# Block compression with stationary blocks over four column strips, and the by-token projection's first unit ahead of the compression's units

## The reference: what is computed

```python
def compress_blocks(k, pe, w1, b1, w2):          # k: (1, 512, 2, 64)
    n_cmp = (T - 32) // 16 + 1                    # 31
    idx = np.arange(n_cmp)[:, None] * 16 + np.arange(32)[None, :]
    blocks = k[:, idx] + pe[None, None, :, None, :]
    flat = transpose(blocks).reshape(B, n_cmp, Hkv, 32 * 64)
    return gelu(flat @ w1 + b1) @ w2              # w1: (2048, 64), w2: (64, 64)

h = rms_norm_2(x, g_pre_mix[l])
q_nsa, kv_nsa, g_nsa, qkv_sb, g_merge = split(h @ w_in)
k_cmp, k_slc, k_win = (rope(kv[:, :, n]) for n in (0, 2, 4))
v_cmp, v_slc, v_win = kv[:, :, 1], kv[:, :, 3], kv[:, :, 5]
o_nsa = gated sum of attention over compressed, selected and window keys
```

## Time and profile before

| | us |
|---|---|
| time, median of 3 runs (2902.05 to 2902.65) | 2902.12 |
| profiled execution | 2901.89 |
| its span, first to last instruction | 2900.1 |
| TensorE busy | 2883.0 (99%) |
| VectorE, ScalarE, GpSimd busy | 1833.0, 1275.3, 182.0 |
| compression on TensorE, first layer | 1384.13 to 1391.72 |
| compression on TensorE, second layer | 2159.77 to 2167.36 |

### The profile page before, as it was taken

One profiled execution on the slowest core, in us unless ns is written; L12 is line 12 of the kernel. 1 busy time (PEld: TensorE's weight loads), 2 busy tenths in 40 slices (PEclk: granted clock), 3 DMA queues, 4 the chain that ended last, 5 costly groups with the idle time before them and its releaser, 6 DMA issues.

```text
span 2900.1 us, 38167 instructions
## 1 busy us (share of the span) xinstructions
PE 2883.0 (99%) x14822; PEld 2384.1 (82%) x14822; DVE 1833.0 (63%) x3171; ACT 1275.3 (44%) x2352; POOL 182.0 (6%) x124
## 2 busy tenths in 40 slices
PE   9999999999999999999999999999999999999998
PEld 7888888888888888888888788888888888888886
DVE  6766775356565487734666768775365777677743
ACT  4544443233333344432366644543333765444431
POOL 1000000010000000000101301000030021100000
PEclk9999999999999999999999999999999999999999
DMA  4233323322222223232411132322333112323222
GB/s 168 74 102 95 102 95 97 99 87 80 80 80 87 95 98 99 95 97 93 136 59 45 59 109 79 103 95 95 101 106 112 43 45 73 109 80 102 95 95 73
DMA packets 74725, 263.88 MB, mean 91 GB/s; under 512 B 9008, under 2 KB 9008, under 8 KB 74416
## 3 DMA queue, kind: packets, MB, share of 16 engines
q1 hardware_dynamic: 73680, 258.03, 27.6%
q10 hardware_dynamic: 864, 3.41, 0.3%
HBM read 255.64 MB, written 2.10 MB: 89 GB/s over the span
## 4 chain that ended last, share of the span: by engine, by line
PE 94%; ACT 2%; DVE 2%; issue 1%; POOL 0%; DVEq 0%
PE bank L552 26%; PE bank L559 26%; PE bank L555 26%; PE bank L765 2%; PE bank L629 2%; PE bank L633 2%; PE bank L630 2%; PE bank L744 2%; PE bank L729 1%; PE bank L935 1%; DVE big L2207 1%; PE bank L720 1%; ACT pp L1162 1%; ACT big L1486 1%; PE bank L988 1%
## 5 line engine op out<-in xcount | busy, mean ns | idle before, releaser
L1507 DVE TENSOR_TENSOR wl<-ring,wh 128x512 fp32r<-128x512 f32 (+1 forms) x928 | 637.3, 693 | 782.4 <-ACT wh L1071 777.0
L552 PE MATMUL bank<-xh,wh 128*128 128x512 f32 x2392 | 942.7, 394 | 0.1
L555 PE MATMUL bank<-xh,wl 128*128 128x512 f32 x2392 | 931.7, 390 | 0.0
L559 PE MATMUL bank<-xl,wh 128*128 128x512 f32 x2392 | 903.8, 390 | 0.0
L1071 ACT ACTIVATE wh<-ring 128x512 fp32r<-128x512 f32 (+1 forms) x928 | 569.0, 622 | 683.3 <-PE bank L559 612.6
L552 PEld LDWEIGHTS bank<-xh,wh 128*128 128x128 f32 x2392 | 449.2, 188 | 101.9 <-issue 10.4
L559 PEld LDWEIGHTS bank<-xl,wh 128*128 128x128 f32 x2392 | 449.0, 188 | 94.5
L555 PEld LDWEIGHTS bank<-xh,wl 128*128 128x128 f32 x2392 | 449.4, 188 | 90.9 <-DVE wl L1507 1.1
L552 PE MATMUL bank<-bigr,wh 128*128 128x512 f32 x1024 | 398.8, 389 | 0.1
L555 PE MATMUL bank<-bigr,wl 128*128 128x512 f32 x1024 | 398.4, 389 | 0.0
L559 PE MATMUL bank<-bigr,wh 128*128 128x512 f32 x1024 | 393.4, 389 | 0.0
(11 more groups left out here) (240 smaller groups left out, 2890.0 us busy)
## 6 DMA issues: line engine op xcount, KB each, us to landing
ring<-in_w_up SPq DMA_DIRECT2D x176, 512.0 KB, 3.5
ring<-in_w_down SPq DMA_DIRECT2D x88, 512.0 KB, 3.4
ring<-in_w_in SPq DMA_DIRECT2D x64, 512.0 KB, 3.5
ring<-in_w_ret SPq DMA_DIRECT2D x32, 512.0 KB, 3.4
ring<-in_w_even SPq DMA_DIRECT2D x19, 512.0 KB, 3.5
ring<-in_w_ret_v SPq DMA_DIRECT2D x16, 512.0 KB, 3.4
ring<-in_w_ret_out SPq DMA_DIRECT2D x16, 512.0 KB, 3.5
ring<-in_w_proj SPq DMA_DIRECT2D x16, 512.0 KB, 3.5
```

What stands on the lines that cost most here:

```text
L552: e.matmul(o, K.wh(p, c * 128, 128), oh, start=start, stop=False, skip_group_check=True)
L555: e.matmul(o, K.wl(p, c * 128, 128), oh, start=False, stop=False, skip_group_check=True)
L559: m = e.matmul(o, K.wh(p, c * 128, 128), ol, start=False, stop=stop, skip_group_check=True)
L1507: e.tensor_tensor(K.wl(i, 0, w), K.raw(i), K.wh(i, 0, w).bitcast(F32), ALU.subtract).then_inc(F.lo.tell(("piece", i)), 1)
```

## The change

The roles in the compression are exchanged. The stationary block is now 64x32: one token offset of the 32 blocks, from a block input `cin(i, part)` that VectorE makes beforehand (tokens plus position table, 32 blocks, the last one zero for part 1). The moving operand is 64 columns of `w1`. The four combinations of keys/values and head write four strips of 32 partitions of one PSUM bank, and the parts are summed there. So `w1` is laid out with the units in the order (keys part 0, values part 0, keys part 1, values part 1), and the compression runs in two halves of 64 instructions, by part. The result has the blocks on the partitions; ScalarE copies it (`hb`), TensorE transposes it behind step 1 of the by-token projection (`hidden_turn`), and ScalarE applies gelu with the bias `b1` straight from PSUM (`hidden_act`). The second layer reads rows 0 to 63 and moves from behind step 3 to behind step 4. VectorE's additions on the small sums go.

In the ring the projection's first unit (pieces 0 to 2) now stands ahead of the four `w1` units; its splits stand in ScalarE's list ahead of the copy, and in VectorE's list behind rope 3 (two) and behind the next scaling (one). The half turns keep their places between the `w1` units.

```diff
@@ weights
-    def moving(self, src, u, key, n, per):
+    def moving(self, src, u, key, n, per, second=None):
         self.first[key] = len(self.pieces)
         for k in range(0, DT, per):
+            if k == per and second is not None:
+                second()
             self.unit(...)
-        for i in range(4):
-            W.raw(D[f"w1_{l}"][i], ("w1", l, i))
-        W.moving(D[f"w_tm{l}"], 0, ("tm", l), 280, 3)
+        W.moving(D[f"w_tm{l}"], 0, ("tm", l), 280, 3, lambda: [W.raw(D[f"w1_{l}"][i], ("w1", l, i)) for i in range(4)])
@@ class Kit
+    def cin(self, i, part):
+        return self.big(11424 + (2 * i + part) * S).rearrange("p (n r) -> p n r", r=16)
@@ sync_program
-        turns.update({u + 1: (l, (0, 1)), u + 2: (l, (2,)), u + 3: (l, (3,)), u + 4: (l, (4,)), u + 7: (l, (5, 6))})
+        turns.update({u + 1: (l, (0, 1)), u + 2: (l, (2,)), u + 3: (l, (3,)), u + 4: (l, (4,)), u + 6: (l, (5, 6))})
@@ tensor_program
-        for i in range(2):
-            c = (K.kcr, K.vcr)[i]
...
-            for part in range(2):
-                u = W.raws["w1", l, 2 * i + part]
-                q.wait_ge(K.landed(u), ("unit", u))
-                for n in range(16):
-                    for kv in range(2):
-                        r = slice(64 * kv, 64 * kv + 64)
-                        m = e.matmul(BK[b][r, 32 * part:32 * part + 32], K.slot(u)[r, n * 64:(n + 1) * 64],
-                                     c[r, 2 * part:2 * part + 32, n], start=part == 0 and n == 0, stop=n == 15,
-                                     skip_group_check=True)
-                m.then_inc(F.attn.tell(("cmp", l, i, part), ("unit", u)), 1)
+        for part in range(2):
+            units = [W.raws["w1", l, 2 * part + i] for i in range(2)]
+            for i in range(2):
+                q.wait_ge(F.dve, ("cin", l, i, part))
+                q.wait_ge(K.landed(units[i]), ("unit", units[i]))
+            for n in range(16):
+                for i in range(2):
+                    for kv in range(2):
+                        r, c = slice(64 * kv, 64 * kv + 64), 64 * i + 32 * kv
+                        m = e.matmul(BK[spare[0]][c:c + 32, 0:64], K.cin(i, part)[r, :, n], K.slot(units[i])[r, n * 64:(n + 1) * 64],
+                                     start=part == 0 and n == 0, stop=part == 1 and n == 15, skip_group_check=True)
+            m.then_inc(F.attn.tell(("cmp", l, part), *[("unit", u) for u in units]), 1)
+        def hidden_turn():
...
+            e.transpose(BK[b][0:64, 0:128], K.hb, K.cs("ident")).then_inc(F.attn.tell(("ch", l)), 1)
-        by_token(("tm", l), 280, s, F.act, {3: compressed})
+        by_token(("tm", l), 280, s, F.act, {1: hidden_turn, 4: compressed})
@@ vector_program
+        def block_input(i):
+            src = (K.KC, K.VCB)[i].rearrange("p (n r) -> p n r", r=16)
+            for part in range(2):
+                a = VEC["pe"] + 64 * l + 32 * i + 16 * part
+                pe = bc(K.VC[:, a:a + 16], [[0, 32 - part], [1, 16]])
+                if part:
+                    e.memset(K.cin(i, part)[:, 31, :], 0.0)
+                e.tensor_tensor(K.cin(i, part)[:, 0:32 - part, :], src[:, part:32, :], pe, ALU.add).then_inc(
+                    F.dve.tell(("cin", l, i, part)), 1)
...
+        block_input(1)
         rope(1)
+        block_input(0)
         rope(2)
         times_rs(K.tmp(0), ("n", l, 6), s, ("ra", l, 5))
         rope(3)
+        lo_to(W.first["tm", l] + 1)
         times_rs(K.tmp(1), ("n", l, 7), s, ("ra", l, 6))
+        lo_to(W.first["tm", l] + 2)
         rope(4)
```

More of the change, by code:

```diff
@@ L336, in memory @@
     K.NQT = [K.big(j * S) for j in range(4)]
-    K.KSL, K.KWN, K.KC, K.VCB = K.big(2048), K.big(2560), K.big(3072, 544), K.big(3616, 544)
-    K.kcr, K.vcr = (t.rearrange("p (n r) -> p n r", r=16) for t in (K.KC, K.VCB))
+    K.KSL, K.KWN, K.KC, K.VCB = K.big(2048), K.big(2560), K.big(3072), K.big(3616)
     K.TM = K.big(4160, 1120)
@@ L344, in memory @@
     K.GM = [K.big(11424 + j * S) for j in range(16)]
-    K.ropes = [K.KC[:, 16:528], *K.NQT, K.KSL, K.KWN]
+    K.ropes = [K.KC, *K.NQT, K.KSL, K.KWN]
     K.at_ropes = [0, S, 2 * S, 3 * S, 2048, 2560]
+    K.hb = K.big(20768, 64)
     K.hid, K.gates = K.big(20640, 128), K.big(20896, 96)
@@ L972, in tensor_program @@
         spare = [b for b in (K.place[key] for key in (*(("n", l, "g", m) for m in (2, 3, 4)), ("n", l, 5))) if b > 3]
[L973 to L992 removed]
+        K.place["cb", l], K.place["ch", l] = spare[0], spare[1]
@@ L994, in compressed @@
+        vacated[spare[0]] = [(F.act, ("hb", l))]
+        def hidden_turn():
+            b = K.place["ch", l]
+            q.wait_ge(F.act, ("hb", l))
+            empty(b)
+            e.transpose(BK[b][0:64, 0:128], K.hb, K.cs("ident")).then_inc(F.attn.tell(("ch", l)), 1)
+            vacated[b] = [(F.act, ("gel", l, 1))]
         def compressed():
-            w2 = K.VC[:, VEC["w2"] + 128 * l:VEC["w2"] + 128 * l + 128]
+            w2 = K.VC[0:64, VEC["w2"] + 128 * l:VEC["w2"] + 128 * l + 128]
@@ L1001, in compressed @@
                     empty(4)
-                e.matmul(BK[4][r, 0:31], w2[r, 0:64], K.hid[r, 64:95], start=True, stop=True,
+                e.matmul(BK[4][r, 0:31], w2[:, 0:64], K.hid[0:64, 32 * kv:32 * kv + 31], start=True, stop=True,
                          skip_group_check=True).then_inc(F.attn.tell(("kc", l, kv)), 1)
@@ L1006, in compressed @@
                 for c in (32 * kv, 64 + 32 * kv):
-                    m = e.matmul(BK[5 + kv][c:c + 31, 0:64], K.hid[r, 96:127], w2[r, 64:128], start=True, stop=True,
-                                 skip_group_check=True)
+                    m = e.matmul(BK[5 + kv][c:c + 31, 0:64], K.hid[0:64, 64 + 32 * kv:95 + 32 * kv], w2[:, 64:128],
+                                 start=True, stop=True, skip_group_check=True)
                 m.then_inc(F.attn.tell(("vc", l, kv)), 1)
@@ L1433, in scalar_program, with hidden_act @@
         e.preload_act_table_set("gelu_apprx_tanh_and_others")
[L1434 to L1442, removed]
+        hi_to(W.first["tm", l] + 2)
+        q.wait_ge(F.attn, ("cmp", l, 1))
+        e.activation(K.hb, K.bank(("cb", l))[:, 0:64], ACT.Copy, bias=0.0, scale=1.0).then_inc(F.act.tell(("hb", l)), 1)
+        def hidden_act():
+            q.wait_ge(F.attn, ("ch", l))
+            for i in range(2):
+                e.activation(K.hid[0:64, 64 * i:64 * i + 64], K.bank(("ch", l))[0:64, 64 * i:64 * i + 64], ACT.Gelu_apprx_tanh,
+                             bias=K.vec("b1", 2 * l + i)[0:64, :], scale=1.0).then_inc(F.act.tell(("gel", l, i)), 1)
         def compressed():
@@ L2086, in vector_program @@
         times_rs(K.tmp(0), ("n", l, "g", 0), s, ("ra", l, 0))
[L2087 removed]
+        times_rs(K.VCB, ("n", l, "g", 1), s)
         for r in (1, 2, 3):
@@ L2093, in vector_program @@
         times_rs(K.tmp(4), ("n", l, 5), s, ("ra", l, 4))
+        q.wait_ge(F.dve, ("freed", "n", l, "g", 1))
+        block_input(1)
         rope(1)
+        q.wait_ge(F.dve, ("rope", l, 0))
+        block_input(0)
         rope(2)
-        q.wait_ge(F.dve, ("rope", l, 0))
         times_rs(K.tmp(0), ("n", l, 6), s, ("ra", l, 5))
@@ L2099, in vector_program @@
         q.wait_ge(F.dve, ("rope", l, 1))
+        lo_to(W.first["tm", l] + 1)
         times_rs(K.tmp(1), ("n", l, 7), s, ("ra", l, 6))
+        lo_to(W.first["tm", l] + 2)
         rope(4)
-        for i in range(2):
-            hb, bias = K.hb(i), K.SM[:, 160 + i:161 + i]
-            q.wait_ge(F.act, ("hb", l, i))
-            e.tensor_tensor(bias, hb[:, 0:1], hb[:, 63:64], ALU.add).then_inc(F.dve.tell(("hbias", l, i)), 1)
-            q.wait_ge(F.dve, ("hbias", l, i))
-            e.tensor_tensor(bias, bias, K.vec("b1", 2 * l + i), ALU.add).then_inc(F.dve.tell(("hbias1", l, i)), 1)
-            e.tensor_tensor(K.hid[:, 32 * i:32 * i + 31], hb[:, 1:32], hb[:, 32:63], ALU.add).then_inc(
-                F.dve.tell(("hid", l, i)), 1)
         e.memset(K.kcc, 0.0)
```

9 lines of the change are left out of this document (3 added, 6 removed).

## The result

The changed kernel takes 2915.28 us (median of 5 runs, 2912.95 to 2916.91) against 2902.26 (5 runs, 2902.05 to 2903.04): a ratio of 1.0045 with a 95% interval of [1.0034, 1.0055]: slower, by little but clear of the scatter. The forecast was 2912.5. The profiled execution took 2914.93 us, 13.0 more than the one of before.

What follows compares the result with a forecast made beforehand. The prediction took TensorE's instruction stream, busy 99% of the span, as the bound. 2901.9 + 5.0 (late sends) + 0.6 (transposes) + 5.0 (clock) = 2912.5 us, range 2904 to 2917.

Steps and rivals of the forecast that it cites:

- layer 1 at full rate: First layer's compression: TensorE idles 6.7 us for the fourth unit, so it ends at 1394.6 instead of 1391.72, +2.9 us.
- layer 2 at full rate: Second layer's compression: TensorE idles 5.9 us for the fourth unit, so it ends at 2169.5 instead of 2167.36, +2.1 us.
- The early split had no stall to remove: Split of the projection's first unit: before the change no wait stood on either side of the compression.
- The strips: Compression on TensorE: four strips at once, 14.5 ns a record instead of 30, 1.9 us a half instead of 3.8.
- Rival B: Strips don't run together, or records stay 30 ns apart: 2916.3 us, or 2916.9 one block at a time; chance 0.20.
- some 7 us longer: Sum if different row tiles could not use one PSUM bank at the same time; the prediction did not adopt that rule.
- The send that waits: Ring: fourth compression unit waits for VectorE's third split behind rope 3; sent 1388.7, 7.1 us later, and 2163.4 in layer two.
- VectorE's additions at nothing: Block inputs and clears on VectorE, 2.7 us per layer ahead of rope 3, costed at nothing because VectorE idled there.
- The transpose: Added TensorE transpose and tile-shape change: 0.3 us per layer, bounds 0.1 to 0.6, +0.6 in all; projection's fourth piece unaffected.
- The clock: TensorE falls to 1.2 GHz in both holes, 2.5 us each, +5.0; bounds 0 and 2 x 4.4.
- rival A: Hole is there but the clock holds, or falls in one layer only: 2907.5 or 2910 us; chance 0.20.
- Rival C: Fourth unit isn't late, its slot coming free before rope 3's turn matters: 7.0 us gained, 2894.9 us; chance 0.07.

Runs made afterwards that it cites:

- E4: Changed kernel plus 24 idle matmuls, results unused, between the compression's halves in each layer: 2908.78 us, 1.0022 of the kernel before.
- E2: Four-strip compression alone, with the ring order, split places and last half turn's place of the kernel before: 2900.40 us, 0.9994 of that kernel.
- E6: E5 with the loop order changed so that two strips, each over its own row half, run before the other two: 2902.22 us.
- E7: E5 with the loop order changed so that the two strips over the same rows run together: 2902.74 us.
- E1: Changed kernel with VectorE's three splits of the projection's first unit put ahead of rope 2: 2903.59 us, 0.9998 of the kernel before.
- E9: E5 with VectorE's splits back at the changed kernel's late place: 2903.83 us, 1.0007 of the kernel before.
- E10: The changed kernel run once more, unaltered, for a second trace: 2912.76 us, 1.0037 of the kernel before.
- E8: E1 with SyncE sending the projection's second unit only when the compression is done: 2900.63 us, 0.9995 of the kernel before.
- E5: E1 with the compression's second half moved behind the projection's step 2, transpose and second layer behind steps 3 and 5: 2896.47 us, 0.9979 of the kernel before.
- E3: New ring order and split places alone, with the old 64 by 64 compression blocks: 2913.26 us, 1.0037 of the kernel before.

## Why the prediction was right, and where it was not

The outcome came by the mechanism forecast: a late send in each layer, an idle TensorE, and a lower clock behind it. That the total came so near is in part luck: in the traces the second layer and the break were 4.1 us more than forecast, and the other terms 1.7 less. **The whole difference in the two traces**, in stretches (full-rate half: the 2.08 us from start to start in E4):

| term | predicted | traces |
|---|---|---|
| layer 1 at full rate (8.02 to the second half + 2.08 - 7.59) | +2.9 | +2.5 |
| layer 2 at full rate (9.71 + 2.08 - 7.59) | +2.1 | +4.2 |
| clock: two second halves of 3.58 instead of 2.08, and nine matmuls | +5.0 | +4.0 (3.0 and 1.0) |
| break in the second half of layer 1 | none | +2.0 |
| transposes and remainder | +0.6 | +0.3 |
| sum | +10.6 | +13.0 |

*The early split had no stall to remove*: right; E2 shows that it gets one only with the short compression.

*The strips*: 14.5 ns a record predicted, 15 measured, 28 with two at a time (E6, E7), so load and pass side by side over the four strips set the price and there is no floor at 30. Rival B is out. The half takes 2.08 us up to the next work, not 1.9 (E4). The page of the Trainium skill "TensorE: Matmul & The Clock Gate" ("Wait — 56ns, not 53.3ns?") puts the least distance at about 25 ns; the change's 128 records in 2.14 us disagree. So does the rule of the Trainium skill's "TensorEngine Tiling (Array Packing)" (Restrictions and Gotchas) that different row tiles cannot use one bank at a time: all strips write one bank, and E6's pair in different row halves ran as fast as E7's in the same rows. The "some 7 us longer" that the prediction gives for that rule does not follow from its own working: the slower first halves would have ended inside the holes, and rival B has the same slowdown at 3.8 us.

*The send that waits*: right in its whole chain. In the first layer it was sent 0.8 us before the forecast (1387.89, not 1388.7), since rope 3's sum came at 1385.42 instead of 1386.2, without the wait for GpSimd that stood ahead of it before. E1 moved the split, and the hole shrank from 5.88 to 1.15 us. **The step that missed** is "In the second layer the scaling stood at 2161.54 ...: sent 2163.4", 3.63 us after the compression's start: it was 5.18. I took the half turn's issuing from before, 2.41 us; in the change one of rope 2's four issues took 2.4 us by itself. The 1.55 us pass straight to the end, and with them 0.2 of a slower landing (4.4 us instead of 4.2). Not all of it need come from that issue: in E4 and E9 the four took 2.41 us, and the send still came 4.21 and 4.25 us after the compression's start, 0.6 later than forecast. What held the issue is open. Slow ones are no rarity: rows 9 have one in their 3.39 us for four (1.58 us by itself), and E10 (3.92 us for the four) and E8 show others.

*VectorE's additions at nothing*: right in the first layer, whose split was early, though the block inputs took 4.0 us there and not 2.7. For the second layer no run separates them from the rest of VectorE's list. *The transpose*: 0.25 a layer (2166.05 - 1397.75 = 768.30, against 768.05), bounds held; no wait stood at the projection's fourth piece.

*The clock*: it falls in both holes, so rival A is out; E4 puts clock and break together at 6.0 us. The size was taken from the kernel's start, 2.5 a hole, and the second layer has just that. What it costs is what runs before it is back: 1.5 for each second half, and 1.0 of projection only in the second layer, since in the first the clock recovered inside the break. The Trainium skill's rule ("TensorE: Matmul & The Clock Gate", Part 1) that an idle TensorE falls to half rate agrees in kind.

*The break* was in none of the steps: I took the instruction stream as always at hand. It was 3.10 us in E1, 1.74 and 1.58 in the change, 0.46 in E2, 0.18 in E8; its cause is open. It is part of why undoing the late split alone (E1) gave only a tie; the rest are the waits of 1.15 and 1.62 us that are left, for E8, with hardly a break, is no clear gain either.

*Rival C* needed a send 2.8 us earlier and a clock that holds: E1 has the send 4.5 us earlier, but not the clock (in its traced run), and ends at the old time; E5, with both, gains 5.9.

## What to carry to other kernels

When a load is put ahead in a ring, price the load that now inherits its slot: it is sent when the slowest reader of the new occupant is done, wherever that reader stands in its engine's list. A shortened stretch is worth its gain only if its data are there; ready work put into the wait (E9) beat filling it with idle matmuls (E4) by 5.0 us at the same late splits, and with the splits early as well (E5) it beat the kernel before by 5.9. And a run of small matmuls can break off, for a reason that no semaphore shows, by up to 3 us; look for idle time put down to "issue".

## What the runs showed of the hardware that was not expected

- Four 32-column strips with both row halves, all writing one PSUM bank, run a record every 15 ns; two at a time 28, over the same rows or not.
- A break of 0.2 to 3.1 us inside the second half when it stands right behind the first: after the 123rd record in the first layer, after the 106th in E2's second layer, nearly none with quiet DMA queues (E8, 1.9% of the engines' time), but none either in E4 with 90%. Its cause is open.
- Holes of 1.15 and 3.10 us one behind the other (E1), or one of 2.55 (E3), let the clock fall to 1.2 GHz as a hole of 5.9 did. The moment varies: 3.3 us after TensorE stopped in the change, 4.6 in E10, 0.8 in E3; in the second layers of E3 and E9 it fell 1.7 and 0.9 us after the work had resumed behind holes of 1.96 and 1.43 us.
- A DMA issue on SyncE of a half turn usually takes 0.59 us; one took 2.4 (E8 has one of 2.5, the kernel before one of 1.9):

```profile
L488 SPq DMA_DIRECT2D pp<-tmp x4: 507/592/2427, 2156.8 to 2160.5; - x4
```
